# Two expert pairs per loop trip on TensorE, with the first four weight pieces of each odd pair in the dense ring

## What is computed

```python
def expert_block(args):
    xb, e = args
    a, b = jnp.split(xb @ w_gu[e], 2, axis=-1)
    return (jax.nn.silu(a) * b) @ w_down[e]
...
gates = pg * pv / jnp.sum(pv, axis=-1, keepdims=True)
expert_id = gi * EXPERTS_PER_GROUP + pi
...
h = h + hier_moe(hn, ...)
```

## Time and profile before

| what | value |
|---|---|
| median of 3 runs | 2128.81 us (2124.58 to 2130.39) |
| profiled execution, its own time | 2130.93 us |
| span of its trace | 2129.1 us |
| mean granted TensorE clock | 0.977 of full speed |
| busy: PE, DVE, ACT | 1997.3, 914.6, 708.8 us |
| moved by DMA | 603.71 MB, mean 284 GB/s |

### The profile page before, as it was taken

One profiled execution on the slowest core, in us unless ns is written; L12 is line 12 of the kernel. 1 busy time (PEld: TensorE's weight loads), 2 busy tenths in 40 slices (PEclk: granted clock), 3 DMA queues, 4 the chain that ended last, 5 costly groups with the idle time before them and its releaser, 6 DMA issues.

```text
span 2129.1 us, 32312 instructions
## 1 busy us (share of the span) xinstructions
PE 1997.3 (94%) x12772; PEld 1449.6 (68%) x12773; DVE 914.6 (43%) x1524; ACT 708.8 (33%) x1109; POOL 80.3 (4%) x119
## 2 busy tenths in 40 slices
PE   7998999999999998889999999999999999999997
PEld 5877899988999897854444444479899444344433
DVE  4876688755653544542222221246555222221212
ACT  3434564254553455521111111144453111111112
POOL 0110211101000200000000000000000000000000
PEclk9999999999999999989999999999998999999999
DMA  9742489802755251479999999935266899999996
GB/s 360 276 145 77 148 300 332 314 30 88 254 189 183 80 172 67 198 317 417 422 422 422 421 422 422 422 123 187 83 214 268 338 422 422 422 422 422 422 422 276
DMA packets 108256, 603.71 MB, mean 284 GB/s; under 512 B 10094, under 2 KB 10548, under 8 KB 59012
## 3 DMA queue, kind: packets, MB, share of 16 engines
q1 hardware_dynamic: 96016, 559.91, 66.5%
q0 software_dynamic: 11872, 42.35, 5.5%
q10 hardware_dynamic: 276, 0.13, 0.0%
HBM read 601.27 MB, written 1.05 MB: 283 GB/s over the span
## 4 chain that ended last, share of the span: by engine, by line
PE 61%; DMA 29%; DVE 4%; ACT 3%; issue 2%; SPq 1%; ACTq 0%; DVEq 0%
DMA expert_w<-in_expert_w_gu 26%; PE bank L1017 11%; PE bank L572 10%; PE bank L574 10%; PE bank L573 10%; PE bank L606 3%; PE bank L1029 3%; PE bank L1002 2%; DMA dense_w<-in_ada_w 1%; PE bank L581 1%; PE bank L583 1%; PE bank L582 1%; PE bank L656 1%; DMA dense_w<-in_w_in 1%; ACT w_high L431 1%
## 5 line engine op out<-in xcount | busy, mean ns | idle before, releaser
L1017 PE MATMUL bank<-expert_w,work 128*64 128x512 f32 (+1 forms) x2240 | 459.8, 599 | 51.6 <-DMA expert_w<-in_expert_w_gu 47.0
L1017 PEld LDWEIGHTS bank<-expert_w,work 128*64 128x64 f32 (+1 forms) x2240 | 153.0, 133 | 352.5 <-issue 352.3
L438 DVE TENSOR_TENSOR w_low<-dense_w,w_high 128x2048 fp32r<-128x2048 f32 x112 | 255.8, 2289 | 216.8 <-ACT w_high L431 216.1
L431 ACT ACTIVATE w_high<-dense_w 128x2048 fp32r<-128x2048 f32 x120 | 228.6, 1910 | 306.0 <-DMA dense_w<-in_mlp_w 186.4
L1029 PE MATMUL bank<-expert_w,work 128*64 128x512 f32 (+1 forms) x1120 | 226.7, 595 | 0.0
L2224 DVE TENSOR_TENSOR work<-work,bank 128x512 f32<-128x512 f32 x32 | 22.0, 687 | 392.2 <-ACT work L1512 392.2
L1029 PEld LDWEIGHTS bank<-expert_w,work 128*64 128x64 f32 (+1 forms) x1120 | 70.0, 132 | 136.4 <-issue 134.3
L1512 ACT ACTIVATE work<-bank 128x512 f32<-128x512 f32 x32 | 19.1, 598 | 429.0 <-PE bank L1017 429.0
L572 PE MATMUL bank<-u_pairs_mlp,w_high 128*128 128x256 f32 x512 | 144.0, 284 | 1.1 <-issue 1.1
L572 PE MATMUL bank<-hidden_pairs,w_high 128*128 128x256 f32 x512 | 144.9, 283 | 0.0
L573 PE MATMUL bank<-hidden_pairs,w_low 128*128 128x256 f32 x512 | 144.9, 283 | 0.0
(11 more groups left out here) (398 smaller groups left out, 3850.2 us busy)
## 6 DMA issues: line engine op xcount, KB each, us to landing
expert_w<-in_expert_w_gu SPq DMA_DIRECT2D x256, 1024.0 KB, 23.0
expert_w<-in_expert_w_down SPq DMA_DIRECT2D x128, 1024.0 KB, 19.2
dense_w<-in_mlp_w SPq DMA_DIRECT2D x64, 1024.0 KB, 5.7
dense_w<-in_ret_w_in SPq DMA_DIRECT2D x24, 1024.0 KB, 5.2
u<-in_ada_w POOLq DMA_DIRECT2D x40, 512.0 KB, 6.7
work<-in_ada_w POOLq DMA_DIRECT2D x40, 512.0 KB, 6.7
dense_w<-in_fox_w_in SPq DMA_DIRECT2D x16, 1024.0 KB, 5.1
dense_w<-in_w_in SPq DMA_DIRECT2D x12, 1024.0 KB, 7.7
```

The source lines that it names most:

```text
L431: nc.scalar.activation(HIGH_OF[at], dense_w[:, at % RING], ACT.Copy, scale=scale).then_inc(S("w_high_ready"), 1)
L438: ins = nc.vector.tensor_tensor(w_low[:, at % RING], dense_w[:, at % RING], high, ALU.subtract)
L1017: last = mm(free[half][cols, :], rows[:, k, cols], pieces[:, k // 2, a, k % 2, half * 512:(half + 1) * 512], start=k == 0, stop=k == KT - 1)
```

## The change

- TensorE's loop body now holds two pairs, an even and an odd one (`one_pair` twice), and runs 7 trips; pairs 14 and 15 stand behind the loop as straight code. The loop carries `hint_back_edge=True`, which puts a BRANCH_PREFETCH_HINT at its head for the branch at its end.
- The pieces of places 0 and 1 of an odd pair go to the four chunks of `dense_w` (`piece_of`), everything else stays in `expert_w`. So places 0 and 1 of pair i+1 can be loaded once pair i-1 has used its own; SP's loop loads places 0 and 1 of pair i+1 and then places 2 to 5 of pair i. Places 0 and 1 of pair 1 are loaded ahead of the loop.
- In layer 0 places 3 and 4 of pair 0 are loaded earlier, after two tiles of the last Fox step. The first four chunks of `ret_in` are loaded at the end of layer 0's loop instead of before it, and the row of gains at the end of layer 1's.
- The last pair has no gather, no take_xg, no build_pick and no weigh; on TensorE its `add_up` stands ahead of the transposes. ScalarE and VectorE run 15 trips and one written-out pair.
- `few` takes the second expert's count for pair 1 as it did for pair 0, so that neither is ever swapped.

```diff
+        def piece_of(odd, j, a):
+
+            return dense_w[:, 2 * j + a] if odd and j < RING // 2 else pieces[:, j, a]
...
+            for x in range(2):
+                wait_tile(sp, TILES["fox_attn"] + fox_tile(FOX_HEADS // 2 - 1, x))
+            for j in (3, 4):
+                load_experts(0, 0, j)
             for l in range(DEPTH):
 
                 wait_tile(sp, TILES["ret_out" if l else "fox_out"] + 7)
-                for j in range(3 if l == 0 else 4, PIECES // 2):
+                for j in range(4 if l else 5, PIECES // 2):
                     load_experts(l, 0, j)
+                for j in range(RING // 2):
+                    load_experts(l, 1, j, 1)
+                sp.wait_ge(S(f"more_known_{l}"), 1)
+                with sp.Fori(0, PAIRS // 2 - 1) as two:
+                    for odd in range(2):
+                        i = 2 * two + 1 + odd
+                        swap = sp.value_load(more_i[0:1, ds(i + 3 * PAIRS, 1)], min_val=0, max_val=1)
+                        swap_next = sp.value_load(more_i[0:1, ds(i + 1 + 3 * PAIRS, 1)], min_val=0, max_val=1)
+                        for j in range(PIECES // 2):
+                            sp.wait_ge(expert_used, PIECES * (PAIRS * l + i - 1) + 2 * j + 2)
+                            if j < RING // 2:
+                                load_experts(l, i + 1, j, odd, swap_next)
+                            else:
+                                load_experts(l, i, j, 0, swap)
+                swap = sp.value_load(more_i[0:1, ds(4 * PAIRS - 1, 1)], min_val=0, max_val=1)
+                for j in range(RING // 2, PIECES // 2):
+                    sp.wait_ge(expert_used, PIECES * (PAIRS * (l + 1) - 2) + 2 * j + 2)
+                    load_experts(l, PAIRS - 1, j, 0, swap)
...
                 if l == 0:
                     for j in range(RING):
+                        sp.wait_ge(expert_used, PIECES * (PAIRS - 1) + 2 * (j // 2) + 2)
                         load(chunk("ret_in", 0, j))
...
+                    if last:
+                        pending(count)
+                        add_up().then_inc(S("added"), 1)
+                        pe.wait_ge(S("hidden_e"), n + 1)
+                        turn_hidden(S("hidden_turned"))
+                        pe.wait_ge(S("pick_w_ready"), n + 1)
+                        turn_pick(pick_w, S("pick_turned"))
+                        pe.wait_ge(S("hidT_ready"), n + 1)
...
+                with nc.Fori(0, PAIRS // 2 - 1, engines=bass.OrderedEngineSet([pe.engine]), hint_back_edge=True) as two:
+                    for odd in range(2):
+                        one_pair(2 * two + odd, two, odd)
+                for odd in range(2):
+                    one_pair(PAIRS - 2 + odd, PAIRS // 2 - 1, odd, last=odd == 1)
```

More of the change, by code:

```diff
@@ L511, in _ @@
[L511 to L516, removed]
                     for q in range(4):
@@ L1007, in experts, with project @@
                             LARGE: [(slice(UNIT * x, UNIT * (x + 1)), int(x == 3)) for x in range(4)]}
-                def project(rows, loaded, used=None, first=SLOTS, late=None):
+                def project(rows, two, odd, used=None, first=SLOTS, late=None):
                     for k in range(KT):
@@ L1013, in project @@
                             pe.wait_ge(S("xg_dve"), late)
-                        both_in(k, loaded)
+                        both_in(k, two, odd)
                         for half in range(2):
                             for cols, a in tiles_of[first]:
-                                last = mm(free[half][cols, :], rows[:, k, cols], pieces[:, k // 2, a, k % 2, half * 512:(half + 1) * 512],
+                                last = mm(free[half][cols, :], rows[:, k, cols], piece_of(odd, k // 2, a)[:, k % 2, half * 512:(half + 1) * 512],
                                           start=k == 0, stop=k == KT - 1)
@@ L1021, in project, with down @@
                     return last
-                def down(loaded, used=None, first=SLOTS):
+                def down(two, odd, used=None, first=SLOTS):
                     for f in range(4):
-                        both_in(KT + f, loaded)
+                        both_in(KT + f, two, odd)
                         for half in range(2):
@@ L1074, in experts, with one_pair @@
                 pe.wait_ge(S(f"more_known_{l}"), 1)
-                with pe.Fori(0, PAIRS) as i:
+                def one_pair(i, two, odd, last=False):
                     n = PAIRS * l + i
-                    loaded = 16 * (n + 1)
                     count = (PAIRS + 1) * l + i + 1
@@ L1107, in experts @@
                         with pe.If(first_rows == first):
-                            project(xg, loaded, expert_used, first, late=count)
-                    pe.wait_ge(S("pick_ready"), count + 1)
-                    pending(count)
-                    for half in range(2):
-                        gather(half, pick).then_inc(S("gathered"), 1)
-                    pe.wait_ge(S("hidden_e"), n + 1)
-                    turn_hidden(S("hidden_turned"))
-                    pe.wait_ge(S("pick_w_ready"), count)
```

100 lines of the change are left out of this document (64 added, 36 removed).

## The result

| | us |
|---|---|
| before, median of 4 runs | 2128.31 (2124.58 to 2130.39) |
| changed kernel, median of 4 runs | 2245.03 (2242.52 to 2246.86) |
| ratio, 95% interval | 1.0549, 1.0534 to 1.0563 |
| changed kernel, profiled execution: time, span | 2245.92, 2244.1 |

What follows compares the result with a forecast made beforehand. The full DMA stream was taken to bound late pairs, costing TensorE 2.7 us of waiting each. Terms -5.4 - 6.5 - 2.0 + 8.2 + 8.5 = +2.8 on 2130.93 gave 2133.7, stated as 2133 us, range 2113 to 2195.

Steps and rivals of the forecast that it cites:

- I take one exposed fetch per trip: TensorE's expert loop: one code fetch of 4.26 us shows in each of 7 trips, costing 8.2 us in all beyond lead.
- Rival 2: TensorE's loop: two exposed fetches per trip, the branch back and one over the further rounds; 2193 us, chance 0.29.
- lead: Time TensorE without DMA would be ahead of pair 15's weight gate, free for stalls: 25.8 and 25.6 us per layer.
- The gate moves by one pair: Late expert pairs: the last w_gu wait becomes pair 14's instead of pair 15's; gain 2.7 us per layer, 5.4 in all.
- the obvious reading: Expert weight stream: 4 MB loaded ahead would take 9.9 us off each layer; not forecast, used as upper bound.
- Last pair without a gather: Pair 15: down starts about 3.15 us after project instead of 6.39; gain 3.2 us per layer, 6.5 in all.
- Entry of layer 0: Before layer 0's first project: code fetch meets idle DMA engines, shortening the 4.26 us gap; gain 2.0 us.
- Straight pairs 14 and 15: Behind the loop: branches over parts not yet fetched cost half of 4.26 us each, 8.5 us in all.
- Signs: Expected in the profile: DMA waits 29.8 us apart, q8 packets every trip, gaps about 4 us, two-pair period 58.6.

Runs made afterwards that it cites:

- the straight version: Changed kernel with all 16 pairs of TensorE written out, no loop, the part for further rounds in each: 2174.03 us, ratio 1.0203.
- the 2111 us run: Changed kernel with TensorE's part for further rounds left out and all 16 pairs in its loop, 8 trips: 2111.25 us, ratio 0.9913.
- the long loop alone: Kernel before with only TensorE's expert loop made 8 trips of two pairs with the hint; no ring, old order of loads: 2251.96 us, ratio 1.0576.
- the last experiment: Kernel before, one pair per trip, with the last pair leaping over its gather and adding first: 2125.03 us, ratio 0.9977.
- the run with the shorter body: Changed kernel with the part for further rounds left out of TensorE's program, pairs 14 and 15 still straight: 2130.29 us, ratio 1.0001.

## Why the prediction was wrong

**The step that failed** is "I take one exposed fetch per trip, at the full 4.26 ... 8.2 us in all". That the body would not stay loaded was right. Its price was too small in three ways.

- *Number:* per trip the branch back waits (3.42 us median) and so does the leap behind it (3.07), and together they show as 5.5 to 7.9 us in layer 0; the straight version shows that the leap alone still costs 2 us per pair, and a third branch, over the wide project, shows as about 1.1 us at the gather. Rival 2 had two of them. In layer 0 the gaps come to 64.5 us, 9.2 per trip, against the 4.26 forecast.
- *Clock:* the sum had no term for what follows a gap. It is 5.3 of the 12.6 us of the trip shown, and some 25 of the 92 in layer 0.
- *Sum:* I had 4.26 x 7 = 29.8 us per layer against 25.7 us of lead, so 4 us left over. Measured are (67.4 - 54.3) x 7 = 92 us: three times the size, against the same 25.7 of lead, and 59.2 us left over in layer 0 after the gains of the end. Rival 2, with 59.6 us per layer and 2193, had the mechanism: its gaps were nearly of the right size (64.5), and what it lacked was the clock.

The range ended at 2195, just past Rival 2, with the tail of more exposed fetches left out; the time was there.

**Point by point**, with the 2111 us run (all pairs in the loop, short body) as the change without the cost of its code:

- *The gate moves by one pair, 2.7 us per layer:* right. The last wait is pair 14's, ending at 1347.96, which is 417.4 us after the first project; before it was 1353.96 - 934.83 = 419.1. From first project to the end of pair 15's project: 448.4 against 452.7, so 4.4 us in layer 0, 2.7 of it the forecast and 1.7 a stream that stands a little earlier. In layer 1 the same stretch gave 1.9 (449.5 against 451.4). The 9.9 of the obvious reading did not come in either. In the changed kernel itself the term is worth nothing, since TensorE sets the pace there.
- *Last pair without a gather, 3.2 us per layer:* a little less. Down starts 3.7 us behind project in that run (1382.62 - 1378.90), 3.5 (1449.84 - 1446.33) in the changed kernel, for 3.15 forecast. Against 6.39 before that is a gain of 2.7, and 2.8 in layer 1.
- *Entry of layer 0, 2.0 us:* right, and a little too small. Kernels with the old order of loads have gaps of 4.26, 4.83 and 4.79 us there (before, the long loop alone, the last experiment); those with the new order and the same leap have 1.54, 2.12 and 1.72 (changed, without the hint, all written out). From 925 to 929 us the DMA share is 1.02 before and 0.02 in the changed kernel. So the full queues account for some 2.8 us of the gap, as read. The gap is gone altogether in the run with the short body, which has no such leap; that run's entry is therefore no measure of the order of loads.
- *Straight pairs 14 and 15, 8.5 us in all:* the right order, and too small. In the changed kernel one leap shows per layer, before pair 14, with 4.41 and 4.07 us, and none before pair 15; pair 14's project behind it takes 15.65 us for 13.73, so 12.3 us in all. In the run with the shorter body, which has no such leap, they cost about as much at another place, behind pair 14's project: 6.0 us per layer there and 1.1 in pair 15 of layer 0, 13 us in all; moving them into the loop brought 14 us in the spans (2128.8 to 2114.9) and 19 in the medians (2130.29 to 2111.25).
- *Signs:* q8 packets on every trip and a long gap before one project in two came as forecast, the gaps at 5.3 to 8.2 us over the two layers and not 4. The DMA waits 29.8 us apart did not appear at all, which was the sign of the forecast being wrong, and TensorE's two-pair period was 67.4, past both the 58.6 and Rival 2's 62.8.

Without the code the gains forecast were 13.9 us. Measured are 14.2 in the spans of the profiled executions (2129.1 to 2114.9) and 18 in the medians (2129.14 to 2111.25). The close match of the spans is partly luck: the terms came to 6.3 (gate), 5.5 (last pair) and 4.3 (entry, of which the order of loads gives some 2.8), 16.1 together, and 1.9 were lost elsewhere.

The size of the code memory that the prediction cited holds: the Trainium skill, "Runtime: NRT & Kernel Launch", section "Instruction fetch mechanics", gives TensorE 2,048 instructions. The runs agree: some 2,030 stay loaded and 2,057 do not. The same section's rule is that only a window of two blocks counts and that a taken branch out of it stalls. That branches to code not loaded stall, the runs bear out (3.07 and 3.42 us); that only two blocks stay, they do not: with a body of 1,815 instructions, some seven packets, the branch back goes over all of it in each trip, and q8 has no packet from 1000 to 1350 us.

## What to carry to other kernels

Count the instructions of a loop's body before making it longer, code that is leapt over included: on TensorE nothing was fetched again up to some 2,030, and from 2,057 the two-pair loop lost nearly 60 us per layer. How much is lost beyond the limit goes by the taken branches: those to code not loaded took 3 to 4 us in the median, of which up to 3 showed where one stood alone (more ahead of the wide pairs) and up to 8 where two followed each other. Rows behind the gap ran at a lower clock, so price a gap here at 1.4 to 1.5 times its length (92 us for 64.5 of gaps in layer 0, 90 for 59.7 in layer 1). Straight code fetched all the time, with its leaps over the wide project, was cheap, not free: 19 us over the two layers. If a rare case makes the body too long, give it a loop of its own and choose once, ahead of the loop; and keep the last, special turn of a loop inside it with a short leap rather than written out behind it.

## What the runs showed that I had not expected

- Pair 14, written out behind the loop, cost more than its instructions: 2.9 us at issue and 3.1 of slow rows in each layer. The place behind a loop is not what it takes. The gap stands where the wide project is leapt over, and with no loop at all a gap of 2.8 to 3.0 us stands at that place in four pairs, pair 14 of layer 1 among them, and not pair 14 of layer 0. What the pairs with such a gap have in common was not found.
- The hint cuts the gaps in layer 0 to about half (5.5 to 7.9 against 12.8 to 14.6 us), but hardly in layer 1 (5.3 to 8.2 against 6.7 to 9.2). Left open.
- The limit is sharp and counts instructions: a body of some 2,030 is fetched once, as one of 1,060 is.
- The instruction packets hardly slow the stream: with the loop gone and 27 of them in 300 us it moves 419 GB/s in place of 422.
